# Sandwich norms of a hybrid block: token scale behind the gate and up products, weighted sums between passes, last product by tokens

## What is computed

```python
def rmsnorm(x, w, eps=NORM_EPS):
    xf = x.astype(jnp.float32)
    y = xf * lax.rsqrt(jnp.mean(xf * xf, axis=-1, keepdims=True) + eps)
    return (y * w.astype(jnp.float32)).astype(x.dtype)
...
    mixed = jax.nn.sigmoid(p_gate_a) * y_a + jax.nn.sigmoid(p_gate_b) * y_b
    x = x + rmsnorm(mixed.astype(x.dtype) @ w_out, norm_mix_post)

    xn = rmsnorm(x, norm_ffn_pre)
    hidden = jax.nn.silu(xn @ ffn_w_gate) * (xn @ ffn_w_up)
    return x + rmsnorm(hidden @ ffn_w_down, norm_ffn_post)
```

## Time and profile before

| | us |
|---|---|
| median of 3 runs | 2225.74 (2225.69 to 2225.81) |
| profiled execution, device time | 2224.51 |
| span of the profiled execution, first to last instruction | 2222.8 |
| PE busy in the span | 2092.7 |
| DVE busy | 1420.4 |
| ACT busy | 1089.3 |

### The profile page before, as it was taken

How to read it: one execution, slowest core, us unless ns; L and a number is a source line. 1 busy time by engine, 2 the same in 40 slices (tenths; PEclk the granted TensorE clock), 3 DMA queues, 4 the chain that set the end, 5 groups by cost and what they waited for, 6 DMA issues and landing times. The chain is left out here.

```text
span 2222.8 us, 49299 instructions
## 1 busy us (share of the span) xinstructions
PE 2092.7 (94%) x20515; PEld 1808.3 (81%) x20515; DVE 1420.4 (64%) x2816; ACT 1089.3 (49%) x2051; POOL 160.3 (7%) x277
## 2 busy tenths in 40 slices
PE   5999999999999999999999999499999999999995
PEld 5888888888888888888888889478888888778884
DVE  5568777777877877787787775544544445444444
ACT  4545554655555565555555545434444444344443
POOL 3001011011011101101110110000000000000000
PEclk9999999999999999999999999799999999999998
DMA  7654444545444455444544435175555555545542
GB/s 203 172 142 125 119 122 122 145 120 129 128 126 124 118 131 135 122 124 119 144 119 120 116 111 162 43 246 187 188 189 189 189 189 189 178 161 186 185 186 86
DMA packets 386637, 327.27 MB, mean 147 GB/s; under 512 B 11697, under 2 KB 334225, under 8 KB 379793
## 3 DMA queue, kind: packets, MB, share of 16 engines
q1 hardware_dynamic: 372384, 318.53, 48.8%
q10 hardware_dynamic: 14064, 6.04, 1.1%
HBM read 322.44 MB, written 2.10 MB: 146 GB/s over the span
## 5 line engine op out<-in xcount | busy, mean ns | idle before, releaser
L247 PE MATMUL ps<-hi_all,xh 128*128 128x384 f32 (+1 forms) x1568 | 564.0, 360 | 31.7 <-ACT pu L273 28.9
L1736 DVE TENSOR_TENSOR lo_all<-stage,hi_all 128x1024 fp32r<-128x1024 f32 x264 | 323.3, 1225 | 385.3 <-ACT hi_all L1731 385.3
L249 PE MATMUL ps<-hi_all,xl 128*128 128x384 f32 (+1 forms) x1568 | 531.8, 339 | 0.0
L248 PE MATMUL ps<-lo_all,xh 128*128 128x384 f32 (+1 forms) x1568 | 530.7, 338 | 0.0
L1731 ACT ACTIVATE hi_all<-stage 128x1024 fp32r<-128x1024 f32 x264 | 279.9, 1061 | 433.7 <-PE ps L1749 427.3
L242 DVE TENSOR_TENSOR lo_all<-stage,hi_all 128x768 fp32r<-128x768 f32 (+1 forms) x400 | 377.9, 965 | 120.5 <-ACT hi_all L237 119.7
L237 ACT ACTIVATE hi_all<-stage 128x768 fp32r<-128x768 f32 (+1 forms) x400 | 327.7, 833 | 217.6 <-PE ps L249 210.9
L247 PEld LDWEIGHTS ps<-hi_all,xh 128*128 128x128 f32 x1568 | 295.8, 189 | 67.6 <-ACT pu L273 36.2
L248 PEld LDWEIGHTS ps<-lo_all,xh 128*128 128x128 f32 x1568 | 296.8, 189 | 0.9
L249 PEld LDWEIGHTS ps<-hi_all,xl 128*128 128x128 f32 x1568 | 296.4, 189 | 0.9
L1745 PE MATMUL ps<-hi_all,xh 128*128 128x512 f32 x704 | 276.8, 393 | 10.0 <-DVE lo_all L1736 10.0
(11 more groups left out here) (277 smaller groups left out, 2655.3 us busy)
## 6 DMA issues: line engine op xcount, KB each, us to landing
stage<-in_w_in SPq DMA_DIRECT2D x288, 512.0 KB, 5.7
stage<-in_ffn_w_gate SPq DMA_DIRECT2D x44, 1024.0 KB, 5.2
stage<-in_ffn_w_up SPq DMA_DIRECT2D x44, 1024.0 KB, 5.2
stage<-in_ffn_w_down SPq DMA_DIRECT2D x22, 2048.0 KB, 7.6
stage<-in_w_out SPq DMA_DIRECT2D x16, 344.0 KB, 4.3
stage<-in_w_out SPq DMA_DIRECT2D x8, 516.0 KB, 4.6
stage<-in_w_in SPq DMA_DIRECT2D x8, 448.0 KB, 6.9
stage<-in_w_out SPq DMA_DIRECT2D x8, 336.0 KB, 4.6
```

Of the source, the lines that this page charges most:

```text
L247: nc.tensor.matmul(o, xh[:, kc, xs], high, start=kc == 0, stop=False)
L248: nc.tensor.matmul(o, xh[:, kc, xs], low, start=False, stop=False)
L249: return nc.tensor.matmul(o, xl[:, kc, xs], high, start=False, stop=kc == KC - 1)
L1736: nc.vector.tensor_tensor(wlo[s.par], src, whi[s.par].bitcast(F32), ALU.subtract).then_inc(s.lo, 1)
```

## The change

1. `scaled`. Between the column groups of the last pass, DVE multiplies each summed group by the gain row into a new tile `scaled` (`out_scale_dve`). The new tile `late` of 17 KB for each partition holds it; in the mixers' block the same memory holds several small tiles of the units, and later tanh, gate and hidden.
2. The second block of the program is gone. What it did is at the head of the third one and in its first block of quanta: the first reciprocal root, then the new x by groups of 256 channels (`new_x`: `scaled` times the token's scale plus `x1`, two instructions for a group), transposes of the new x itself, not yet scaled (`turn_x`, into banks 4 to 7), and `high` and `low` as before. Groups 0 to 2 come ahead of quantum 0, the others between quanta.
3. The second norm's token scale is applied behind the products. Squares of the new x and the reciprocal root stand behind quantum 8 of the first block (`second_norm`). The tanh takes half the scale as its factor, and the product with up takes half its square; as such a factor is one number for each token, both run once for each token tile in all 11 blocks.
4. The first four loads of gate weights are issued in the mixers' block, and quantum 0 is split there.
5. The last of the 22 steps of the last product runs all of token tile 0 and then all of tile 1, its columns in the order 2, 3, 0, 1, with two more buffers for split weights (the unused rest of `hi_all` and `lo_all`, and rows of `xh` and `xl`). The last norm runs by token tiles: gain by column groups straight from PSUM, squares on ACT, reciprocal root, then scale and residual in halves of 1024 columns, each followed by its own transfer of 512 KB.

```diff
+        late = sb("late", [P, 17 * T])
+        scaled = late[:, 0:2 * D].rearrange("p (t n) -> p t n", t=NT)
...
+        def out_scale_dve(dve, p):
+            if p == 0:
+                dve.wait_ge(row_in, 16)
+            dve.wait_ge(out_sum, p + 1)
+            cs = slice(OAT[p], OAT[p] + OW[p])
+            nc.vector.tensor_tensor(scaled[:, :, cs], part[:, :, cs], row[:, cs].unsqueeze(1).to_broadcast([P, NT, OW[p]]),
+                                    ALU.mult).then_inc(out_scaled, 1)
...
+                    if p == OP - 1:
+                        act.wait_ge(ffn_landed[0], 16)
+                        act.wait_ge(quantum_done, QALL + OQ + 4)
+                        stage_hi(act, 0, 0, ffn_quantum(0))
                     out_square_act(act, p)
...
+                    out_scale_dve(dve, p)
+                stage_lo(dve, 0, 0, ffn_quantum(0))
...
+                    for f, split in enumerate((OQ, OQ + 4, OQ + 4, OQ + OP)):
+                        sp.wait_ge(lo_ready, QALL + split)
+                        load_ffn(sp, 0, f)
...
+        whi.append(xh[:, 0:4, :].rearrange("p (k a) n -> p k (a n)", k=2))
+        wlo.append(xl[:, 0:4, :].rearrange("p (k a) n -> p k (a n)", k=2))
...
-                sp.wait_ge(V.sem, V.after("a1"))
-                sp.dma_start(out[0].rearrange("(t p) n -> p t n", p=P), y2).then_inc(result_out, 16)
-                sp.wait_ge(result_out, 16)
+                for t in range(NT):
+                    for h in range(2):
+                        sp.wait_ge(V.sem, V.after(f"y{t}{h}"))
+                        cs = slice(h * D // 2, (h + 1) * D // 2)
+                        sp.dma_start(out[0][t * P:(t + 1) * P, cs], y2[:, t, cs]).then_inc(result_out, 16)
+                sp.wait_ge(result_out, 64)
...
+                def high(g):
+                    transpose_x_act(act, A, E, NORM2, range(g, g + 1), 4)
                 def block_act(jb, first):
                     for q in range(QF):
-                        if q % 2 == 0:
-                            act.wait_ge(S.landed[(q // 2) % 4], jb * 32 + 16 * (q // 8 + 1))
-                        stage_hi(act, S, jb * QF + q, quantum(q))
+                        if not (first and q == 0):
+                            if q % 2 == 0:
+                                act.wait_ge(ffn_landed[(q // 2) % 4], jb * 32 + 16 * (q // 8 + 1))
+                            stage_hi(act, jb * QF + q, q % 2, ffn_quantum(q))
+                        if first and q == 1:
+                            high(0)
+                            high(1)
+                        if first and 1 <= q <= 6:
+                            high(q + 1)
+                        if first and q == 8:
+                            for t in range(NT):
+                                act.wait_ge(V.sem, V.after("x7"))
+                                if t:
+                                    act.wait_ge(A.sem, A.after("ss0"))
+                                A.step(f"ss{t}", nc.scalar.activation(scaled[:, 0, :], x2[:, t, :], ACT.Square,
+                                                                      accum_out=ssx[:, t:t + 1]))
                         if q == 3 and not first:
                             store(jb - 1)
                         if q == 9:
-                            act.wait_ge(S.used, jb * QF + QF // 2)
-                            nc.scalar.activation(tg_[:], ps[:, 0:2, :], ACT.Tanh, scale=0.5).then_inc(tanh_done, 1)
+                            act.wait_ge(ffn_used, jb * QF + QF // 2)
+                            if first:
+                                act.wait_ge(V.sem, V.after("half"))
+                            for t in range(NT):
+                                last = nc.scalar.activation(tg_[:, t, :], ps[:, t, :], ACT.Tanh, scale=half_rs[:, t:t + 1])
+                            last.then_inc(tanh_done, 1)
...
+                down_act(JD - 2, 0, QE - NB, 8 * JD)
+                act.wait_ge(ffn_used, QE - NB)
+                nc.scalar.activation(hh[1][:], hidT[:, 2 * JD - 2:2 * JD, :], ACT.Copy).then_inc(left_hi, 1)
+                act.wait_ge(down_in[1], 8 * JD)
+                for b in (2, 3, 0, 1):
+                    if b < 2:
+                        act.wait_ge(ffn_used, QE - 1 + b)
+                    nc.scalar.activation(whi[b], down_quantum(1, b), ACT.Copy).then_inc(ffn_hi, 1)
                 for t in range(NT):
+                    act.wait_ge(down_sum, t + 1)
                     for b in range(NB):
                         if t + b:
-                            act.wait_ge(A.sem, A.after(f"sq{t * NB + b - 1}"))
-                        A.step(f"sq{t * NB + b}", nc.scalar.activation(tg_[:, 0, :], ps[:, 2 * b + t, :], ACT.Square,
-                                                                       accum_out=sq4[:, t, b:b + 1]))
+                            act.wait_ge(down_square, NB * t + b)
+                        if b >= 2:
+                            act.wait_ge(V.sem, V.after(f"w{t}{b}"))
+                        nc.scalar.activation(sink, ps[:, 2 * b + t, :], ACT.Square, accum_out=ssy[:, t, b:b + 1]
+                                             ).then_inc(down_square, 1)
...
+                def new_x(g):
+                    cs = slice(2 * P * g, 2 * P * (g + 1))
+                    for t in range(NT):
+                        last = nc.vector.scalar_tensor_tensor(x2[:, t, cs], scaled[:, t, cs], rr[:, t:t + 1], x1[:, t, cs],
+                                                              ALU.mult, ALU.add)
+                    V.step(f"x{g}", last)
+                def low(g):
+                    transpose_x_dve(dve, V, A, NORM2, range(g, g + 1), 4)
                 def hidden(jb):
-                    dve.wait_ge(S.used, jb * QF + QF)
-                    nc.vector.scalar_tensor_tensor(hid[:], gg[:], 0.5, ps[:, 2:4, :], ALU.mult, ALU.mult
-                                                   ).then_inc(hidden_done, 1)
+                    dve.wait_ge(ffn_used, jb * QF + QF)
+                    for t in range(NT):
+                        last = nc.vector.scalar_tensor_tensor(hid[:, t, :], gg[:, t, :], gate_rs[:, t:t + 1], ps[:, 2 + t, :],
+                                                              ALU.mult, ALU.mult)
+                    last.then_inc(hidden_done, 1)
...
+                    V.step("half", nc.vector.tensor_scalar(half_rs[:], rr[:], 0.5, None, ALU.mult))
+                    done("half")
+                    V.step("gate", nc.vector.tensor_tensor(gate_rs[:], half_rs[:], rr[:], ALU.mult))
+                    done("gate")
                 def block_dve(jb, first):
                     for q in range(QF):
-                        stage_lo(dve, S, jb * QF + q, quantum(q))
+                        if not (first and q == 0):
+                            stage_lo(dve, jb * QF + q, q % 2, ffn_quantum(q))
+                        if first and q == 1:
+                            low(1)
+                            new_x(3)
+                        if first and 2 <= q <= 7:
+                            low(q)
+                            if q < 6:
+                                new_x(q + 2)
+                        if first and q == 8:
+                            second_norm()
...
+                rsqrt(nc, dve, V, "p", 0, rr[:], ssx[:], rtm[:])
+                dve.wait_ge(x1_in, 16)
+                new_x(0)
+                new_x(1)
+                low(0)
+                new_x(2)
...
+                down_dve(JD - 2, 0, QE - NB)
+                left(JD - 1, 1)
+                for i, b in enumerate((2, 3, 0, 1)):
+                    stage_lo(dve, QE + i, b, down_quantum(1, b))
                 dve.wait_ge(row2_in, 16)
-                dve.wait_ge(A.sem, A.after(f"sq{2 * NB - 1}"))
-                post_norm_dve(dve, V, sq4[:], lambda t: ps[:].rearrange("p (n t) c -> p n t c", t=NT)[:, :, t, :],
-                              y2, x2, y2)
+                for t in range(NT):
+                    one = slice(t, t + 1)
+                    dve.wait_ge(down_sum, t + 1)
+                    for b in (3, 2, 0, 1):
+                        if b < 2:
+                            dve.wait_ge(down_square, NB * t + b + 1)
+                        cs = slice(CB * b, CB * b + CB)
+                        V.step(f"w{t}{b}", nc.vector.tensor_tensor(y2[:, t, cs], ps[:, 2 * b + t, :], row[:, cs], ALU.mult))
+                    dve.wait_ge(down_square, NB * t + NB)
+                    V.step(f"sum{t}", nc.vector.tensor_reduce(ssx[:, one], ssy[:, t, 0:NB], AX.X, ALU.add))
+                    done(f"sum{t}")
+                    V.step(f"var{t}", nc.vector.tensor_scalar(ssx[:, one], ssx[:, one], 1.0 / D, NORM_EPS, ALU.mult, ALU.add))
+                    done(f"var{t}")
+                    rsqrt(nc, dve, V, f"r{t}_", 0, rr[:, one], ssx[:, one], rtm[:, one])
+                    done(f"w{t}1")
+                    for h in range(2):
+                        cs = slice(h * D // 2, (h + 1) * D // 2)
```

(17 more changed lines are left out.)

240 lines of the change are left out of this document (99 added, 141 removed).

## The result

| | before | after |
|---|---|---|
| median, us | 2225.74 (2225.69 to 2225.81) | 2196.11 (2195.41 to 2200.3) |
| span of the profiled execution | 2222.8 | 2194.2 |
| last matmul to the end of the span | 24.7 | 13.6 |

The ratio is 0.987, with a 95% interval from 0.9856 to 0.9884: faster by 29.6 us, where 25.5 were forecast. Four runs of the changed kernel lie 4.9 us apart.

What follows compares the result with a forecast made beforehand. PE is busy 2092.7 of 2222.8 us, so gains lie only in its holes at the 26th slice and the tail. Head 15.2 + tail 10.4 - loop 0.1 = 25.5 us, from 2225.7 to 2200.2 us; range 2196.0 to 2205.5.

Steps and rivals of the forecast that it cites:

- rival (a): Ahead of quantum 9: the clock doesn't fall in the hole, since PE worked without rest before; 2198.1 us, chance 0.13.
- Parts 1 and 2: Head, up to the barrier and then quantum 0: first root begins at 1416.0, quantum 0 ends at 1428.6.
- Part 3: Quanta 1 to 8: PE needs 3.15 us each, DVE's order is a second bound; quantum 8 ends at 1454.9.
- Part 4: Ahead of quantum 9: squares and second root make PE stand still 4.0 us; with the slow clock, head gains 15.2 us.
- clock term of 2.1: Slow clock restart behind the hole ahead of quantum 9: 2.1 us taken, with 0 and 2.9 as ends.
- Rival (b): Head: clock stays low through quanta 0 to 3 or more; 2204 to 2211 us, chance 0.11.
- Part 5: Gate and up loop: split tanh and up products are covered by idle time, except 0.1 us behind the last block.
- Part 6: Tail: last transfer starts 10.0 us behind the last matmul and takes 3.5 us; the tail gains 10.4 us.
- rival (c): Loop: split tanh and up products run past their cover, making it slower than before; 2252 us, chance 0.01.
- rival (d): Head: early loads come late, so ACT and the barrier wait 5.2 us for a landing; 2205.4 us, chance 0.03.

Runs made afterwards that it cites:

- `both`: Changed kernel with second-norm squares and root spread over quanta 8 to 13, plus DVE taking `low` and new x before the rest of the weights in quanta 2 to 7: 2189.45 us.
- `head_only`: Changed kernel with the tail of the kernel before (no token tiles, one 2 MB transfer): 2210.73 us, against 2225.24 for the kernel before.
- `long_hole`: Changed kernel with one more pass of squares on ACT in quantum 8, lengthening PE's wait ahead of quantum 9: 2201.0 us.
- `one_transfer`: Changed kernel with the result written by one transfer of 2048 KB instead of four of 512 KB: 2200.77 us.

## Why the prediction was right, point by point

**The result** of 2196.11 lies 0.1 above the lower edge of the range (2196.0 to 2205.5), 4.1 below the forecast and outside the span of times that got 0.70; the second measurement of the same kernel, 2197.77, lies inside that. The forecast's mechanism was right; of the outcomes it named, the first execution followed rival (a), with a span of 2194.2 against 2197.3. That the result is inside the range is luck in part. The edge doesn't follow from its own bounds: rival (a) at 2198.1, less 14 times 0.13, less 1.9 for a transfer of 1.6 us, gives 2194.4.

**Parts 1 and 2** held: root 1415.6 (1416.0), quantum 0 from 1423.65 (1423.9). It ended at 1427.4 instead of 1428.6, after 3.8 us, as the clock was up sooner. In the second trace its 12 matmuls took 5.1 us, on the other side of the 4.7 I took; both happen.

**Part 3** held in size and in pattern: of every two quanta one waits, for DVE's order, and `both` shows this by taking the wait away. Quantum 8 ended at 1454.6 (1454.9).

**Part 4** is the step that was mis-sized. The hole was 3.4 us (4.0): from the squares to quantum 9 it took 8.2 us (8.3), and quantum 8 ended 4.7 behind their start (4.3). The clock term of 2.1 was 0 in one trace and 1.5 in three. So the head gained 18.3 in the first trace, not 15.2, and from the last `w_out` matmul to quantum 10 it gained 17.9 there and 15.1 in the second, where the clock fell; in `head_only` the medians give 14.5. Rival (a), which I gave 0.13, deserved more: the nearest row was a wait of 4.07 us, and 3.4 is not the same. The rule of the Trainium skill (TensorE: Matmul & The Clock Gate, HAM oscillation), that a loop whose matmuls wait between bursts starts every burst slow again, was borne out by three traces of four, and by `long_hole`.

**Rival (b)**, a clock low through quanta 0 to 3, didn't come in any trace: it was at full speed by quantum 1 in all of them, over the transposes and short waits.

**Part 5** held. The 0.8 us given back in the first trace are mostly scatter: from quantum 10 to the last up matmul the eleven traces with split tanh and product take 462.7 to 463.7 us, the two without 463.2. What comes in every trace that ends the loop as before is 0.18 us at the last block (7.12 or 7.13 us instead of 6.94), for the 0.1 of the sum. The pair of tanh took 1.25 us instead of 1.01, more than the 0.1 I took, and the idle time covered it. The 45.5 us that I gave for a block of the loop was wrong: it is 44.7 in the kernel before and after.

**Part 6**: the last issue came 10.0 us behind the end of the last matmul, as worked out step by step, and PE didn't wait in the last step. The landing took 2.7 us instead of 3.5; I had scaled it from loads, which are slower than this write. Tail gain 11.1 instead of 10.4. By the Trainium skill (DMA: Bandwidth & Descriptors, Anatomy of one DMA) the estimate was 3.2; the trace has less, and the trace decides. `one_transfer` puts the four pieces at 3.7 of the 11.1 us.

Four figures are slightly off without effect: 12 x 0.43 is 5.2, 1459.0 - 1454.9 is 4.1, the restart behind 10.00 us cost 1.5 (4.28 - 2.74), and rival (c) comes to 2251. Rival (c) is excluded by the loop, rival (d) by the split of quantum 0 at 1412.76, which waited for no load.

## What to carry to other kernels

A scale that is one number for each row of the result can go behind the product, but the work of finding it must then be cut into pieces that fit the engines' idle time between quanta, or it makes a new hole: here 3.4 us, and often 1.5 more for the clock. When such a hole is costed, look in which order each engine takes its queue, and give a clock term both of its values rather than one between them. Look too at each place where PE waits for the last result of a stage, and ask whether the next stage can begin on old results: that edit brought 7 us here, more than the change's second-norm deferral by itself (3.4 or 5.1 by the medians).

## What the hardware did that I had not expected

- After a wait of PE of 3.4 us the clock had fallen in three traces and not in a fourth. After 4.07 us it had fallen in every trace that has that wait, after 5.44 in its one trace.
- Short stretches near half clock stand in the mixers, 6 to 10 by execution, at 1.7 us of full clock each, and their places can differ between executions of the same code. PE was done with `w_out` between 1410.7 and 1414.8 in traces in which that code is the same. Part of the scatter lies there, part in quantum 0 (4.13 to 5.66 us to the start of quantum 1), part in quantum 9, part in the first quantum of the last product (4.36 to 5.26 us behind the same wait of 4.07).
- A write of 512 KB from SBUF landed in 2.7 us, of 2048 KB in 6.4, so 2.5 us for each further MB.
